# Modulation in halves of 256 columns, with weights split into high and low parts, in a decoder layer step

## What is computed

```python
mod = jnp.einsum('bd,de->be', jax.nn.silu(c), w['w_ada']) + w['b_ada']      # (9, 1024) x (1024, 6144)
sh1, sc1, ga1, sh2, sc2, ga2 = jnp.split(mod[:, None, :], 6, axis=-1)
h = _rms(x, w['norm1_g']) * (1.0 + sc1) + sh1
z = h @ w['w_in']
...
g_a, g_b = jnp.split(jax.nn.sigmoid(merge_l), 2, axis=-1)                   # merge_l: last 2048 columns of z
x = x + ga1 * ((g_a * y_a + g_b * y_b) @ w['w_out'])
```

## Time and profile before

| | us |
|---|---|
| median of 3 runs | 2103.25 (2102.1 to 2104.37) |
| the profiled execution | 2101.45, its span 2099.6 |
| TensorE busy | 1984.2 (95% of the span) |
| VectorE busy | 1110.5 (53%) |
| ScalarE busy | 633.9 (30%) |
| POOL busy | 115.9 (6%) |
| chain that ended last, share on TensorE | 42% |

### The profile page before, as it was taken

The page is one execution under the profiler, slowest core; times in us unless marked ns, Lnnn a source line. Parts: engine busy times, 40 slices in busy tenths (PEclk is TensorE's granted clock), DMA queues, the critical chain, the costliest instruction groups (busy, mean ns, idle before and its releaser), DMA issues. The chain is left out here.

```text
span 2099.6 us, 34008 instructions
## 1 busy us (share of the span) xinstructions
PE 1984.2 (95%) x12728; PEld 1813.2 (86%) x12728; DVE 1110.5 (53%) x2492; ACT 633.9 (30%) x1249; POOL 115.9 (6%) x176
## 2 busy tenths in 40 slices
PE   5988999999998798999999999899999999999997
PEld 1328897798998688898898999899999999999997
DVE  0425243243253677777775546655556555555555
ACT  2113343241223466666673133311111010101111
POOL 1013000001300100000200000000000000000000
PEclk9998999999999699999999999999999999999998
DMA  9756453432101000000003531110112121111102
GB/s 319 257 179 213 154 169 101 144 98 67 52 26 66 1 1 1 1 1 1 1 1 103 178 124 55 55 61 30 60 30 60 30 60 31 58 48 42 40 0 81
DMA packets 134205, 157.48 MB, mean 75 GB/s; under 512 B 15619, under 2 KB 102499, under 8 KB 134036
## 3 DMA queue, kind: packets, MB, share of 16 engines
q1 hardware_dynamic: 120622, 129.97, 19.6%
q0 software_dynamic: 4832, 17.15, 2.6%
q10 hardware_dynamic: 8640, 8.89, 1.3%
HBM read 139.53 MB, written 18.54 MB: 75 GB/s over the span
## 5 line engine op out<-in xcount | busy, mean ns | idle before, releaser
L1813 DVE SCALAR_TENSOR_TENSOR l_x2T<-tail_bank,g_modT,l_x2T 128x344 f32<-128x344 f32 (+1 forms) x528 | 265.8, 565 | 103.5 <-PE tail_bank L1551 103.1
L1551 PE MATMUL tail_bank<-l_wo 128*128 128x344 f32 x1584 | 271.8, 321 | 2.8 <-DVE late_total_s L1819 2.8
L1551 PEld LDWEIGHTS tail_bank<-l_wo 128*128 128x128 f32 x1584 | 254.3, 189 | 3.3 <-issue 3.3
L1383 ACT ACTIVATE l_act<-tail_bank 128x344 f32<-128x344 f32 x66 | 30.2, 457 | 523.9 <-PE tail_bank L1533 523.8
L818 PE MATMUL nsa_out<-zs_z,nsa_probT 128*128 128x64 f32 (+1 forms) x1344 | 174.2, 275 | 4.9 <-DVE zs_z L974 4.7
L818 PEld LDWEIGHTS nsa_out<-zs_z,nsa_probT 128*128 128x128 f32 x1344 | 167.0, 196 | 6.9 <-DVE zs_z L974 6.8
L1533 PE MATMUL tail_bank<-late_words_hi,l_uhi 128*128 128x344 f32 x528 | 169.9, 322 | 1.0 <-DVE late_words_lo L1715 1.0
L1533 PE MATMUL tail_bank<-late_words_hi,l_ulo 128*128 128x344 f32 x528 | 169.3, 321 | 0.0
L1533 PE MATMUL tail_bank<-late_words_lo,l_uhi 128*128 128x344 f32 x528 | 169.3, 321 | 0.0
L1533 PE MATMUL tail_bank<-late_words_lo,late_wo 128*128 128x344 f32 x528 | 169.2, 320 | 0.0
L1533 PE MATMUL tail_bank<-late_words_hi,l_wo 128*128 128x344 f32 x528 | 169.2, 320 | 0.0
(11 more groups left out here) (491 smaller groups left out, 4085.3 us busy)
## 6 DMA issues: line engine op xcount, KB each, us to landing
mod_wr<-in_w_ada SPq DMA_DIRECT2D x12, 2048.0 KB, 8.9
kin_kin<-in_cache_kv SPq DMA_DIRECT2D x64, 256.0 KB, 3.5
late_gate<-in_w_ffn_in SPq DMA_DIRECT2D x22, 512.0 KB, 5.9
l_raw_o<-in_w_ffn_out SPq DMA_DIRECT2D x22, 512.0 KB, 3.6
late_raw<-in_w_ffn_in SPq DMA_DIRECT2D x22, 512.0 KB, 5.5
gate_d<-dec_gate ACTq DMA_DIRECT2D x48, 172.0 KB, 2.5
late_gate<-gate_d SPq DMA_DIRECT2D x8, 1032.0 KB, 5.3
dec_raw<-in_w_in POOLq DMA_DIRECT2D x16, 512.0 KB, 5.6
```

Of the source, the lines that this page charges most:

```text
L1383: act.activation(sg[(j + c) % 2], pg[(j + c) % 2][:, 0:TCH], ACT.Silu).then_inc(silu_done, 1)
L1551: mm = pe.matmul(po[u % 4][:, 0:TCH], w[j][:, k * P:(k + 1) * P], a[j][:, tok(c)], start=(q == 0), stop=(q == 2))
L1813: mm = dve.scalar_tensor_tensor(out=here, in0=po[u % 4][:, 0:part_w(c)], scalar=g.modT[:, 5 * KD + k, NDEC:NC9], in1=here, op0=ALU.mult, o ...
```

## The change

In the first stage the modulation works on 24 halves of 256 columns. For each half ScalarE makes a rounded copy `whi`, VectorE the rest `wlo`, and TensorE multiplies both by an 18-column stationary operand `c18` that holds the high and the low part of the 9 conditioning rows side by side. The 18 result rows are copied (`mod_copied`); a small product with `pick`, which adds row j and row 9 + j, turns and sums them; the bias is added after that, from a transposed copy. There are three buffers each of raw weights, `whi` and `wlo`. A raw buffer is free after VectorE's subtraction (`w_lo`). The decode rows are projected in eight pieces of 243 columns. The turning of x goes one group a piece from piece 11 on (`UNIT0`), all k of the first 512 tokens, then of the second; the low part of h is made by POOL. The squares of x stand between ScalarE's copies 1 to 9, the root and `load_constants` behind copy 9. `mod` is not stored any more. The first gate weight is fetched by SP at the end of this stage, into a buffer `graw0` of its own, and POOL fetches the second one first.

```diff
@@ -98,40 +96,50 @@
 def modulation_and_h(nc, io, g):
 
 
-    ZC = 486
+
+    WC = 256
+    NMOD = 6 * D // WC
+    ZC = ZW // 8
     NZ = ZW // ZC
+    RAWS, SPLITS = 3, 3
+    RATE, UNIT0 = 8, 11
...
+                for m in range(NMOD + NZ):
+                    if m >= RAWS:
+                        old = m - RAWS
+                        if old < NMOD:
+                            sp.wait_ge(w_lo, old + 1)
+                        else:
+                            sp.wait_ge(z_ps, old - NMOD + 1)
+                    if m < NMOD:
+                        sp.dma_start(wr[m % RAWS][:], w_ada[:, :, m * WC:(m + 1) * WC]).then_inc(w_in[m % RAWS], 16)
                     else:
-                        c = (n - NMOD) * ZC
-                        sp.dma_start(wr[n % 3][:, :, 0:ZC], w_z[:, :, c:c + ZC]).then_inc(w_in[n % 3], 16)
+                        c = (m - NMOD) * ZC
+                        sp.dma_start(wr[m % RAWS][:, :, 0:ZC], w_all[:, :, c:c + ZC]).then_inc(w_in[m % RAWS], 16)
+                sp.dma_start(g.graw0[:], w_all[:, :, C_M:C_M + P]).then_inc(g.graw_in, 16)
...
+                def low_h(u):
+                    half, k = half_of(u), k_of(u)
+                    cols = slice(half * 512, half * 512 + 512)
+                    pool.wait_ge(h_hi, u + 1)
+                    pool.tensor_tensor(g.hT_lo[:, k, cols], hf[:, u % 3, :], f32(g.hT_hi[:, k, cols]), ALU.subtract).then_inc(h_lo, 1)
+
+                for u in range(2 * KD):
+                    low_h(u)
...
+                def shifted(u):
+                    if u is not None:
+                        k = k_of(u)
+                        act.wait_ge(h_ps, u + 1)
+                        act.wait_ge(coef, 1)
+                        if u >= 3:
+                            act.wait_ge(h_lo, u - 2)
+                        act.activation(hf[:, u % 3, :], pt[u % 3][:], ACT.Identity, bias=g.modT[:, k, NDEC:NC9],
+                                       scale=aT[:, k, NDEC:NC9]).then_inc(h_sb, 1)
+
...
+                for m in range(NMOD):
+                    loaded(act, m)
+                    if m >= SPLITS:
+                        act.wait_ge(mod_ps, m - SPLITS + 1)
+                    act.activation(whi[m % SPLITS][:], wr[m % RAWS][:], ACT.Copy).then_inc(w_hi, 1)
+                    if 1 <= m <= TT + 1:
+                        if m > 1:
+                            act.wait_ge(sq_done, m - 1)
+                        square(m - 1)
+                    if m == TT + 1:
+                        act.wait_ge(rstd_done, 1)
+                        act.activation(rstd[:], rstd[:], ACT.Sqrt).then_inc(std_done, 1)
+                        load_constants(act, io, g)
+                    shifted(unit_at(m))
+                for m in range(NMOD, NMOD + NZ):
+                    shifted(unit_at(m))
...
+                def turned(u):
+                    if u is not None:
+                        half, k = half_of(u), k_of(u)
+                        pe.wait_ge(xn_done, 1 + 4 * (half + 1))
                         if u >= 3:
                             pe.wait_ge(h_sb, u - 2)
                         for q in range(4):
                             mm = pe.transpose(pt[u % 3][:, q * P:(q + 1) * P], x[:, half * 4 + q, k * P:(k + 1) * P], g.ident[:])
                         mm.then_inc(h_ps, 1)
+
+                for m in range(NMOD):
+                    pe.wait_ge(w_lo, m + 1)
+                    if m >= 3:
+                        pe.wait_ge(mod_sb, m - 2)
+                    for k in range(KD):
+                        for q, b in enumerate((whi, wlo)):
+                            mm = pe.matmul(pm[m % 3][:], c18[:, k, :], b[m % SPLITS][:, k, :], start=(k == 0 and q == 0), stop=(k == KD - 1 and q == 1))
+                    mm.then_inc(mod_ps, 1)
+                    if m:
+                        mod_transposed(m - 1)
+                    if m == UNIT0:
+                        pe.wait_ge(xn_done, 1)
+                        for k in range(KD):
+                            mm = pe.transpose(pc[:, k, 0:NDEC], xs[:, k * P:(k + 1) * P], g.ident[0:NDEC, 0:NDEC])
+                        mm.then_inc(hs_ps, 1)
+                    turned(unit_at(m))
                 mod_transposed(NMOD - 1)
                 pe.wait_ge(coef, 3)
-                for n in range(NMOD, NMOD + NZ):
-                    pe.wait_ge(w_in[n % 3], n // 3 * 16 + 16)
-                    if n < NMOD + 3:
-                        pe.wait_ge(mod_sb, n - 2)
+                for i in range(NZ):
+                    m = NMOD + i
+                    loaded(pe, m)
+                    if i < 3:
+                        pe.wait_ge(mod_sb, min(NMOD, NMOD + i - 2))
                     else:
-                        pe.wait_ge(z_sb, n - NMOD - 2)
+                        pe.wait_ge(z_sb, i - 2)
                     for k in range(KD):
-                        mm = pe.matmul(pm[n % 3][0:NDEC, 0:ZC], hs[:, k, :], wr[n % 3][:, k, 0:ZC], start=(k == 0), stop=(k == KD - 1))
-                    mm.then_inc(mod_ps, 1)
+                        mm = pe.matmul(pm[m % 3][0:NDEC, 0:ZC], hs[:, k, :], wr[m % RAWS][:, k, 0:ZC], start=(k == 0), stop=(k == KD - 1))
+                    mm.then_inc(z_ps, 1)
...
+                def mod_copied(m):
+                    dve.wait_ge(mod_ps, m + 1)
+                    if m >= 2:
+                        dve.wait_ge(modT_ps, m - 1)
+                    dve.tensor_copy(mod[m % 2][:], pm[m % 3][:]).then_inc(mod_sb, 1)
...
+                for m in range(NMOD):
+                    dve.wait_ge(w_hi, m + 1)
+                    dve.tensor_tensor(wlo[m % SPLITS][:], wr[m % RAWS][:], f32(whi[m % SPLITS][:]), ALU.subtract).then_inc(w_lo, 1)
+                    if m >= 1:
+                        mod_copied(m - 1)
+                    if m >= 2:
+                        mod_biased(m - 2)
+                    if m == RATE + 1:
+                        dve.wait_ge(modT_sb, RATE)
                         dve.scalar_tensor_tensor(out=aT[:], in0=g.modT[:, KD:2 * KD, :], scalar=1.0,
                                                  in1=g.gT[:, 0:KD].unsqueeze(2).broadcast_to([P, KD, NC9]), op0=ALU.add, op1=ALU.mult).then_inc(coef, 1)
-                    if n == FIRST - 1:
-
                         dve.wait_ge(sq_done, TT + 1)
                         dve.tensor_scalar(rstd[:], ssq[:], 1.0 / D, EPS, ALU.mult, ALU.add).then_inc(rstd_done, 1)
                         dve.wait_ge(std_done, 1)
                         dve.reciprocal(rstd[:], rstd[:]).then_inc(rstd_done, 1)
                         dve.wait_ge(rstd_done, 2)
-                        dve.tensor_scalar(xs[:], xs[:], rstd[0:NDEC, TT:TT + 1], None, ALU.mult).then_inc(xn_done, 1)
-                        for t in range(TT):
-                            dve.tensor_scalar(x[:, t, :], x[:, t, :], rstd[:, t:t + 1], None, ALU.mult).then_inc(xn_done, 1)
-                    for u in units(n):
-                        k, half = u // 2, u % 2
-                        dve.wait_ge(h_sb, u + 1)
-                        hi = g.hT_hi[:, k, half * 512:(half + 1) * 512]
-                        lo = g.hT_lo[:, k, half * 512:(half + 1) * 512]
-                        dve.tensor_copy(hi, hf[u % 2][:]).then_inc(hs_st, 1)
-                        dve.wait_ge(hs_st, u + 1)
-                        dve.tensor_tensor(lo, hf[u % 2][:], f32(hi), ALU.subtract).then_inc(h_split, 1)
-                    if n == FIRST:
-
-                        dve.wait_ge(hs_ps, 1)
-                        dve.wait_ge(coef, 1)
-                        dve.tensor_tensor(hs[:], pc[:, :, 0:NDEC], aT[:, :, 0:NDEC], ALU.mult).then_inc(coef, 1)
...
+                mod_copied(NMOD - 1)
+                for m in range(NMOD - 2, NMOD):
+                    mod_biased(m)
+                for i in range(NZ):
+                    dve.wait_ge(z_ps, i + 1)
+                    dve.tensor_copy(g.zd[:, i * ZC:(i + 1) * ZC], pm[(NMOD + i) % 3][0:NDEC, 0:ZC]).then_inc(z_sb, 1)
+                    high_h(unit_at(NMOD + i))
...
@@ -2044,7 +2109,6 @@
                         pool.wait_ge(raw_free, n - 1)
                     pool.dma_start(raw[n % 2][:], w[:, :, C_M + n * P:C_M + (n + 1) * P]).then_inc(w_in[n % 2], 16)
 
-                load_weights(0)
                 load_weights(1)
                 pool.memset(g.wcmp[:], 0.0).then_inc(cst, 1)
                 pool.memset(ones[:], 1.0).then_inc(cst, 1)
@@ -2373,7 +2437,10 @@
 
                 def split(n):
                     j = n % 2
-                    dve.wait_ge(w_in[j], n // 2 * 16 + 16)
+                    if n == 0:
+                        dve.wait_ge(g.graw_in, 16)
+                    else:
+                        dve.wait_ge(w_in[j], (n + 1) // 2 * 16)
                     if n >= 2:
                         dve.wait_ge(acc_full, 3 * (n - 1))
                     dve.tensor_copy(whi[j][:], raw[j][:]).then_inc(w_hi, 1)
```

(26 more changed lines are left out.)

150 lines of the change are left out of this document (73 added, 77 removed).

## The result

| | before | after |
|---|---|---|
| median, us (runs) | 2102.68 (2100.12 to 2104.37, 4) | 2180.56 (2179.21 to 2185.87, 4) |
| span of the profiled execution, us | 2099.6 | 2179.1 |
| TensorE busy, us | 1984.2 | 1995.1 |
| VectorE busy, us | 1110.5 | 1159.5 |

The ratio is 1.037, with a 95% interval from 1.035 to 1.039. The changed kernel is 78 us slower, where 73 us were forecast. The loss lies in the first stage (83.7 us); 5.9 us of it come back at the gates. One execution of a later kernel, the one with the shift two halves later, took 4940.59 us; it counts in that kernel's median of 2104.18 us (2103.65 without it) and not in its ratio.

A forecast was written before the change was run, and what follows sets the result against it. TensorE was taken to bound the stage; the new order makes serial turns at the lower clock. First stage +79.8 less gate fetch 6.5 gives +73.3 on 2103.25: 2177 us, range 2146 to 2192.

The forecast's parts named there:

- tail and projection, end: End of first stage: 1.6 us of tail, then the decode projection in eight pieces, ending at 228.4 against 148.56 us.
- What bounds the kernel before: First stage: TensorE works without a gap from 23.35 to 148.56 us; no other engine has to be fast.
- The new order: ScalarE's shift of group m-11 stands before the next copy, so from m = 11 to 23 halves do not overlap.
- Which clock: TensorE stands still 5.0 us each turn, so matmuls run at 1.2 GHz; transposes may get the higher clock back.
- rival B: Serial turns of the first stage with the clock kept at 2.4 GHz: 7.9 us a turn, 2152 us; chance 0.20.
- One turn: Copy, subtraction, matmuls, `mod_transposed`, turning, shift and handovers in series: 10.0 us at 1.2 GHz, 7.9 at 2.4; 9.7 taken.
- The rule on transposes: Transposes do not count as TensorE activity as matmuls do; a turn would be 10.0 us, the total some 4 above.
- The first half: The first weight half shares DMA with 4 MB of x and lands at 21 us, bounds 15 and 23.
- The constants: Twenty DMA issues on ScalarE, 9.7 us, now between copies 9 and 10 with nothing to hide them, ending at 66.1.
- The gate fetch: After the projection: gates start 7.8 us earlier, but queries wait for weight 1's split; gain 6.5 us, bounds 3 and 7.8.
- At nothing: POOL's subtractions: POOL's subtractions, one in a 9.7 us turn under the next copy, were put at no cost.
- Rival C: First-stage turns overlap and buffers set the pace, 3.3 us a half; deciding point is copy m+1's start; 2094 us, chance 0.05.

The follow-up runs named there:

- the run that holds 2.4 GHz: The changed kernel with 18 small float32 identity products, read by nobody, added on TensorE after each group of turning transposes; 2167.35 us, ratio 1.030.
- the kernel with two halves and the constants last: The changed kernel with the shift and high part of h two halves later and `load_constants` at the end of ScalarE's stage list; 2097.20 us, ratio 0.996.
- The best version reached by experiment: The changed kernel with shift two halves later, constants last, and POOL's sixteen subtractions of h given to VectorE; 2094.61 us, ratio 0.995.

## Why the prediction was right, point by point

| step of the prediction | forecast | measured |
|---|---|---|
| first half lands | 21 | 18.65 |
| a half, m = 0 to 9 | 3.3 | 3.2 |
| root ends | 56.4 | 52.7 |
| constants on ScalarE | 9.7 | 9.5 |
| copy 10 to the start of shift 0 | 14.2 | 15.25 |
| one turn | 9.7 (9.5 to 10.0) | 10.18 |
| tail and projection, end | 228.4 | 232.27 |
| gate fetch and what it shifts | -6.5 | -5.9 |
| sum | +73.3 | +77.9 (medians), +79.5 (spans) |

*What bounds the kernel before* was right for this stage, by TensorE's timeline without gaps. The chain of the page doesn't show it: it covers 46% of the span, 42% on TensorE, and lies behind this stage.

*The new order* was read right. It follows from the three lists alone, and the experiment that only moves the shift confirms it. *Which clock* was right as well: the matmuls of every turn ran at 1.2 GHz, and the run that holds 2.4 GHz gives what that costs in the turns, 24 us where rival B had 21.6.

*One turn* was mis-sized by 0.5 us, twelve times over, 6 us in all. Of its terms the copy, the subtraction, the shift and the matmuls (3.52 us with the handover, 3.42 forecast) were near. `mod_transposed` was not: from its start to the turning it took 0.75 us in the turn shown and up to 0.95, where the nearest rows gave 0.34 or 0.45. A turn at the lower clock throughout, from TensorE's timeline of the changed kernel:

```profile
125.83 1.02 PE L247 MATMUL mod_pq<-mod_pick,mod_mod 18*128 18x9 f32 x4
126.78 1.11 PE L257 MATMUL mod_pt<-g_ident,mod_x 128*128 128x128 f32 x4
```

Even at the higher clock it takes 0.54 us (104.17 to 104.71 in the kernel with two halves and the constants last). The nearest rows had 8 or 9 partitions where these have 18; whether that is the cause wasn't tried. The turning ran at 0.66 us in eight of the twelve turns and at 1.11 in four, so turns lasted about 10.0 or 10.6 us. The band of 9.5 to 10.0 had the right width, and was 0.5 too low.

*The rule on transposes* of the Trainium skill, "TensorE: Matmul & The Clock Gate" (Part 4: PE-mode transpose), would have put the turn at 10.0, nearer to the 10.18 than my 9.7, but not for its reason. It would have the turning at the lower clock in every turn. Measured, it ran at the higher, 0.66 us a group, in eight of twelve, behind 3.5 us of matmuls at the lower. So transposes do run at the higher clock here, whatever their part in raising it; that part was not tested.

*The first half* came 2.4 us before the value taken, inside its bounds, and copy 10 started 3.8 us early (62.27 against 66.1). This paid back most of the turns' error of 6 us, and that was luck: without it the sum would have missed by 8 us and not by under 5. That rows of half the length get a smaller share of the DMA fits the traces: the tiles of x landed 12.8 us (median) after their issue beside the 2 KB rows, and 8.1 us beside the 1 KB rows; the pieces were half as large too, so this doesn't show it alone. *The constants* were right to 0.2 us on ScalarE. What the prediction didn't ask is what their DMAs do to the weights that load beside them; the experiments that move them put 3 to 5 us on it.

*The gate fetch* came out as worked: 7.8 us forecast for the start, 8.1 measured (10.9 less 2.77); for the queries 6.5 forecast, 5.9 measured here and 5.7 alone. *At nothing: POOL's subtractions* held for this kernel, one in a turn of 10 us: a single VectorE operation was lengthened, L329 by 1 us. In the faster versions with POOL it fails.

*Rival C* named the right point of decision, but its pace of 3.3 us left out VectorE. By the rows above a half takes VectorE 3.06 us without the low part of h (87.22 to 90.28) and 3.67 with it, and POOL's taking it over does not help. The best version reached by experiment takes 3.8 us a half and 2094.6 us.

## What to carry to other kernels

A software pipeline is as deep as its instruction lists say, whatever the number of buffers. Follow the waits of one step round all engines: if the first engine's next step stands behind a wait for the last engine's result of this step, the buffers are idle and the turn is the sum of all engines' times; two steps of skew in the lists were needed here, one only let two halves share a turn. Before an order is judged by its total time, read the end of the stage: here a later stage that nobody edited took 12 us more or less, with the granted clock.

## What the runs showed of the hardware that I had not expected

- In these traces VectorE and POOL held each other up on operations that read and write SBUF alone: POOL's 128x512 subtraction took 3.28 us instead of 1.28 beside VectorE's, VectorE's 128x2048 subtraction 3.27 instead of 2.28, a 128x512 cast 1.10 instead of 0.40, and in the changed kernel a 128x64 addition 1.26 us instead of the 0.22 of the same operation before. From the changed kernel's timelines of VectorE and POOL:

```profile
88.59 1.26 DVE L329 TENSOR_TENSOR mod_hs<-mod_hs,g_modT 128x64 f32<-128x64 f32 x1
...
88.50 1.27 POOL L182 TENSOR_TENSOR h_hT_lo<-mod_hf,h_hT_hi 128x512 fp32r<-128x512 f32 x1 [8.39 <-DVE h_hT_hi L322]
```

- Twenty small constant DMAs issued ahead of a 1 MB weight load went with a landing 5.3 us later, and beside the projection with one landing of 9.0 to 9.5 us in each of three kernels, where the slowest took 5.4 to 6.6 us without them.
- The higher clock came back in the middle of a turn in some turns and not in others, behind the same 5.0 us of waiting and 3.5 us of matmuls at the lower level: 8 of 12 turning groups took 0.66 us, 4 took 1.11.
- Two executions of one kernel, with nothing changed, differed by 21 us (2103.30 and 2124.35), the longer one at the lower mean granted clock (0.963 against 0.972).
